# Turning prompt stick-breaking probabilities by a store, a fetch of 32x32 squares and VectorE, where TensorE turned them

## The reference, cut to what matters

```
def _sb_core(q, k, v, qpos, kpos):
    z = jnp.einsum('bqhd,bkhd->bhqk', q, k).astype(jnp.float32) * (SB_HD ** -0.5)
    valid = kpos[None, :] < qpos[:, None]
    log_beta = jax.nn.log_sigmoid(z)
    log_rem = jnp.where(valid, jax.nn.log_sigmoid(-z), 0.0)
    later = lax.cumsum(log_rem, axis=3, reverse=True) - log_rem
    a = jnp.where(valid, jnp.exp(log_beta + later), 0.0).astype(v.dtype)
    return jnp.einsum('bhqk,bkhd->bqhd', a, v)
...
    o = (o.reshape(b, s, SB_W) * jax.nn.silu(g)) @ w_out
```

## Time and profile before

| | |
|---|---|
| median of 3 runs | 806.83 us (806.25 to 807.87) |
| profiled execution, its own time | 809.91 us |
| span of the profiled execution | 808.1 us |
| TensorE busy | 775.6 us, 96% |
| VectorE busy | 548.2 us, 68% |
| ScalarE busy | 393.4 us, 49% |
| GpSimd busy | 207.7 us, 26% |

### The profile page before, as it was taken

The page is one execution under the profiler, slowest core; times in us unless marked ns, Lnnn a source line. Parts: engine busy times, 40 slices in busy tenths (PEclk is TensorE's granted clock), DMA queues, the critical chain, the costliest instruction groups (busy, mean ns, idle before and its releaser), DMA issues.

```text
span 808.1 us, 16622 instructions
## 1 busy us (share of the span) xinstructions
PE 775.6 (96%) x6364; PEld 679.1 (84%) x6364; DVE 548.2 (68%) x1086; ACT 393.4 (49%) x903; POOL 207.7 (26%) x301
## 2 busy tenths in 40 slices
PE   6999999999999998999999999999999999999895
PEld 5997788888889987778999988888888888777674
DVE  4476366666677669776923666776577777878778
ACT  3234533444534445332324556675567565687710
POOL 2020323211311231001340332233222343662003
PEclk9999999999999999999999999999999999999999
DMA  7632222311725354423243434334433444344113
GB/s 238 153 95 82 71 61 80 85 42 42 153 66 134 93 143 126 147 68 116 79 126 97 113 109 130 107 107 129 130 107 107 129 118 125 109 130 143 62 40 131
DMA packets 63869, 87.29 MB, mean 108 GB/s; under 512 B 8944, under 2 KB 48656, under 8 KB 63792
## 3 DMA queue, kind: packets, MB, share of 16 engines
q1 hardware_dynamic: 53216, 61.88, 25.8%
q0 software_dynamic: 10576, 24.34, 11.7%
HBM read 75.29 MB, written 10.90 MB: 107 GB/s over the span
## 4 chain that ended last, share of the span: by engine, by line
PE 72%; issue 10%; DVE 9%; ACT 4%; POOL 3%; DMA 2%; DVEq 0%; SPq 0%; ACTq 0%; POOLq 0%
PE turn L1020 26%; PE pair L1020 16%; PE value L1020 13%; PE proj L1020 10%; PE turn L1069 2%; POOL rstd L993 1%; POOL k_c L925 1%; DVE probs L1789 1%; PE proj L1231 1%; PE turn L1231 1%; PE proj L1069 1%; PE value L1069 1%; DVE w_words L1658 1%; PE pair L1069 1%; DVE xT_lo L1663 1%
## 5 line engine op out<-in xcount | busy, mean ns | idle before, releaser
L1020 PE MATMUL turn<-w_words,xT_hi 128*128 128x256 f32 (+2 forms) x696 | 147.4, 308 | 1.9 <-ACT k_n L1583 0.9
L1658 DVE TENSOR_TENSOR w_words<-stage,w_words 128x512 fp32r<-128x512 f32 (+1 forms) x136 | 91.8, 682 | 83.7 <-ACT w_words L1432 83.6
L1020 PEld LDWEIGHTS turn<-w_words,xT_hi 128*128 128x128 f32 x696 | 111.7, 191 | 7.4 <-issue 1.6
L1020 PE MATMUL turn<-w_words,xT_lo 128*128 128x256 f32 (+2 forms) x356 | 106.4, 299 | 0.0
L925 POOL DMA_DIRECT2D k_c<-in_cache_sb_k_dram x128 | 82.8, 655 | 85.3 <-DVE k_cT L1773 79.7
L1432 ACT CAST w_words<-stage 128x512 fp32r<-128x512 f32 (+1 forms) x144 | 87.4, 617 | 29.0 <-DMA stage<-in_w_in_even_dram 14.1
L1020 PE MATMUL turn<-xT_hi,w_words 128*128 128x320 f32 x384 | 90.0, 314 | 0.0
L1020 PE MATMUL value<-w_words,xT_hi 128*128 128x256 f32 (+2 forms) x360 | 79.8, 315 | 1.4 <-DVE w_words L1658 1.3
L1020 PE MATMUL pair<-w_words,xT_hi 128*128 128x512 f32 (+2 forms) x272 | 71.6, 350 | 0.0
L1020 PE MATMUL proj<-w_words,xT_hi 128*128 128x256 f32 (+2 forms) x352 | 69.8, 297 | 0.6 <-DVE uq L1865 0.6
L1020 PEld LDWEIGHTS turn<-w_words,xT_lo 128*128 128x128 f32 x356 | 67.8, 190 | 2.5
(11 more groups left out here) (470 smaller groups left out, 1705.5 us busy)
## 6 DMA issues: line engine op xcount, KB each, us to landing
stage<-in_w_in_odd_dram SPq DMA_DIRECT2D x64, 256.0 KB, 2.8
stage<-in_w_in_even_dram SPq DMA_DIRECT2D x44, 256.0 KB, 3.0
k_c<-in_cache_sb_k_dram POOLq DMA_DIRECT2D x128, 64.0 KB, 2.4
v_c<-in_cache_sb_v_dram SPq DMA_DIRECT2D x32, 256.0 KB, 2.9
mlaK<-in_cache_diff_k_dram POOLq DMA_DIRECT2D x32, 128.0 KB, 3.9
mlaK<-in_cache_diff_v_dram SPq DMA_DIRECT2D x32, 128.0 KB, 3.8
stage<-in_w_out_even_dram SPq DMA_DIRECT2D x16, 256.0 KB, 3.0
stage<-in_w_out_odd_dram SPq DMA_DIRECT2D x16, 256.0 KB, 2.8
```

Of the source, the lines that this page charges most:

```text
L1020: return nc.tensor.matmul(o, l, r, start=first, stop=last)
L1658: v.tensor_tensor(piece(w_lo[:, sec % 2, words]), piece(stage[:, n % STAGES, :]), piece(w_hi[:, sec % 2, words].bitcast(F32)), ALU.subtrac ...
```

## The change

22 prompt steps of groups 0 to 2 (the prompt steps among the first 33 steps: all 8 of groups 0 and 1, and the first 6 of group 2) lose their `turn` and `turn2`. By tile they are 6 steps of tile 3, 5 of tile 2, 5 of tile 1 and 6 of tile 0, together 110 blocks of 128x128. In their place come three jobs: `spill`, in which SP stores the step's probabilities into a scratch area (a part of the output `y_prompt` that is written for good later); `fetch`, in which POOL loads them with four DMAs as squares into the buffer that the turned blocks had, and the queries are dealt out so that row 4r+m goes to column r of block m; and `unpack`, one VectorE transpose in place over both heads. `value` waits for `unpack`, and VectorE's gate product writes its columns back in the queries' order.

```diff
+def through_memory(steps):
+    return [s for s in steps[:33] if s[0] == "B"]
...
         jobs.append(("score", now))
+        if i >= 2 and steps[i - 2] in by_memory:
+            jobs.append(("fetch", steps[i - 2]))
         for bundle in fill[:1]:
             jobs += bundle
-        if i >= 2:
+        if i >= 2 and steps[i - 2] not in by_memory:
             s = steps[i - 2]
             jobs.append(("turn", s))
...
         jobs += later.pop(i, []) + tails.get(i, [])
         if i >= 3:
             s = steps[i - 3]
+            if s in by_memory:
+                jobs.append(("unpack", s))
             jobs.append(("value", s))
...
         if i >= 1:
             jobs.append(("weigh", steps[i - 1]))
+            if steps[i - 1] in by_memory:
+                jobs.append(("spill", steps[i - 1]))
         jobs.append(("stick", now))
...
+                if kind == "spill":
+                    s = job[1]
+                    sp.wait_ge(stick_done, stick_no[s])
+                    sp.dma_start(scratch(s).rearrange("(q h n) -> q h n", q=P, h=2), stick_view(s)).then_inc(spilled[by_memory_no[s] % 4], 16)
...
+                if kind == "fetch":
+                    s = job[1]
+                    pool.wait_ge(spilled[by_memory_no[s] % 4], 16 * ((by_memory_no[s] + 3) // 4))
+                    if stick_no[s] > 2:
+                        wait_filled(pool, ("value", sb_steps[stick_no[s] - 3]))
+                    for e in range(P // SQ):
+                        pool.dma_start(packed(s)[e * SQ:(e + 1) * SQ].rearrange("r (x c) -> r x c", c=SQ),
+                                       scratch(s).rearrange("(r x e c) -> e r x c", r=SQ, e=P // SQ, c=SQ)[e]).then_inc(
+                                           fetched[by_memory_no[s] % 2], 16)
...
-                        wait_drained(pe, ("turn2", s))
+                        if s in by_memory_no:
+                            pe.wait_ge(squares_unpacked, by_memory_no[s])
+                        else:
+                            wait_drained(pe, ("turn2", s))
...
+                elif kind == "unpack":
+                    s = job[1]
+                    dve.wait_ge(fetched[by_memory_no[s] % 2], 16 * (P // SQ) * ((by_memory_no[s] + 1) // 2))
+                    v.transpose(packed(s), packed(s)).then_inc(squares_unpacked, 1)
...
-                    v.tensor_tensor(oT[:, 2 * g + blk, tok(t)], ps(job)[:, 0:P], gT[:, g % 2, blk, tok(t)], ALU.mult).then_inc(done, 1)
+                    o, values, gate = oT[:, 2 * g + blk, tok(t)], ps(job)[:, 0:P], gT[:, g % 2, blk, tok(t)]
+                    if job[1] in by_memory_no:
+                        o, gate = (x.rearrange("p (r m) -> p m r", m=4) for x in (o, gate))
+                        values = values.rearrange("p (m r) -> p m r", m=4)
+                    v.tensor_tensor(o, values, gate, ALU.mult).then_inc(done, 1)
```

More of the change, by code:

```diff
@@ L149, in stick_pipeline @@
     samples = [j for j, s in enumerate(steps) if s[0] == "BS"]
+    by_memory = through_memory(steps)
     for i, now in enumerate(steps):
@@ L593, in trunk_kernel @@
         keys_turned = sem("keys_turned")
+        squares_unpacked = sem("squares_unpacked")
+        spilled = [sem(f"spilled{i}") for i in range(4)]
+        fetched = [sem(f"fetched{i}") for i in range(2)]
         vc_in = [sem(f"vc_in{i}") for i in range(2)]
@@ L633, in turned, with packed, unpacked, scratch @@
             return wT1[:, nth[s] % 2, i, :] if s in stick_no else wT0[nth[s] % 2][i]
+        def packed(s):
+            n = 2 * width(s)
+            return flat(work8).rearrange("p (s n) -> p s n", s=2)[:, nth[s] % 2, 0:n]
+        def unpacked(s, h, j):
+            return packed(s).rearrange("p (m h j r) -> p h j m r", m=4, h=2, r=SQ)[:, h, j]
+        def scratch(s):
+            n = 2 * width(s)
+            base = by_memory_no[s] % 4 * P * D
+            return out[0].rearrange("b t d -> (b t d)")[base:base + P * n]
         def stick_view(s):
@@ L705, in trunk_kernel @@
                 units.setdefault(sec, [j, j])[1] = j
+        by_memory = [j[1] for j in schedule if j[0] == "spill"]
+        by_memory_no = {s: i + 1 for i, s in enumerate(by_memory)}
         stick_no = {s: i + 1 for i, s in enumerate(sb_steps)}
@@ L930, in _ @@
                 kind = job[0]
-                if job == ("uq", S_TILE, 1):
+                if kind == "fetch":
[7 more added lines that the diff above has]
+                                           fetched[by_memory_no[s] % 2], 16)
+                elif job == ("uq", S_TILE, 1):
                     wait_filled(pool, job)
@@ L1243, in _ @@
                     wait_bank(pe, job)
-                    wait_drained(pe, ("turn", s))
+                    if s not in by_memory_no:
+                        wait_drained(pe, ("turn", s))
                     o, w = ps(job), turned(s, 0)
@@ L1286, in _ @@
                                 c0 = (2 * blk + h) * HD
-                                m = mm(o[HD * h:HD * h + HD, 0:P], v_n[:, g % 2, j, c0:c0 + HD],
-                                       wT1[:, nth[s] % 2, h, tok(j)], j == 0, j == last)
+                                weights = unpacked(s, h, j) if s in by_memory_no else wT1[:, nth[s] % 2, h, tok(j)]
+                                m = mm(o[HD * h:HD * h + HD, 0:P], v_n[:, g % 2, j, c0:c0 + HD], weights, j == 0, j == last)
                     else:
@@ L1508, in _ @@
                         last = sb_steps[stick_no[s] - 4]
-                        wait_filled(act, ("turn2" if last[0] == "B" else "turn", last))
+                        if last in by_memory_no:
+                            act.wait_ge(spilled[by_memory_no[last] % 4], 16 * ((by_memory_no[last] + 3) // 4))
+                        else:
+                            wait_filled(act, ("turn2" if last[0] == "B" else "turn", last))
                     wait_filled(act, job)
```

## The result

| | before | after |
|---|---|---|
| median of 4 runs | 807.35 us (806.25 to 809.5) | 892.1 us (890.35 to 893.12) |
| span of the profiled execution | 808.1 us | 891.3 us |
| idle time of TensorE in the 36 steps | 4.0 us | 70.3 us |
| its mean granted clock over the span | 0.998 | 0.953 |

The changed kernel takes 1.1036 times as long (95% interval 1.102 to 1.1051): 84.7 us more, where 50.2 were forecast, and 892.1 us where 857 were, with a range up to 878. Slower was right, and so was the mechanism of the wait, VectorE's queue; the amount wasn't.

What follows compares the result with a forecast made beforehand. TensorE was taken to bound the kernel; +61.6 us of new waits, less 8.4 of turns and 3.0 of old idle time, gave +50.2 on 806.8, so 857 us, range 842 to 878.

Steps and rivals of the forecast that it cites:

- What bounds the kernel: In the 36 steps TensorE works 242.0 of 246.0 us; work removed gains its length, a new wait costs its full length.
- What TensorE loses: In the 22 steps, 110 blocks no longer turned at 0.108 us each: 11.9 us, of which 8.4 counted as kept.
- The wait that is added: Before the 22 values, TensorE waits for VectorE's queue to reach and finish the unpack: 61.6 us of new waiting.
- the sum: Over the 36 steps: +61.6 of waits, -8.4 of turns, -3.0 of old idle time, making +50.2 us.
- The unpack: VectorE's transposes before the 22 values, 1.29 us for tile 3 down to 0.37: 18.3 us, with nothing hiding it.
- Edits costed at nothing: ScalarE's copies, VectorE's added work, strided gate and value products, SP's spill and POOL's fetch: all taken as costing nothing.
- Is the round trip hidden?: Store and fetch for tile 3 take 9.1 us against 12.3 available in step 0: hidden, costing nothing.
- Clock 1.00 in the steps: Expected sign in the profile after: TensorE's granted clock stays at full speed through the 36 steps.
- a rival with a chance of 0.03: Waits of 4 us drop TensorE to 1.2 GHz for the step behind, in 11 steps: +70, 927 us; chance 0.03.

Runs made afterwards that it cites:

- a version that shows it bare: Changed kernel with each unpack moved forward in VectorE's queue, behind the score or the first bundle of the fill: 862.05 us, 1.0661 of before.
- the eleven-step version: Changed kernel with only the 11 steps of tiles 1 and 0 through memory, unpack early, behind the first bundle: 819.19 us, 1.0138 of before.
- the late eleven-step version: Changed kernel with only the 11 steps of tiles 1 and 0 through memory, unpack directly ahead of the value: 851.14 us, 1.0515 of before.
- the early fifteen-step one: Changed kernel with only tiles 1 and 0 plus steps 0, 3, 12 and 15 through memory, unpacks early: 830.21 us, 1.0265 of before.

## Why the prediction was wrong, step by step

- **What bounds the kernel.** Right. Leaving the turns out gave nearly microsecond for microsecond (13.7 for 11.9 + the idle time), and each new wait cost at least its full length.
- **What TensorE loses**, 0.108 us a block, 11.9 in all. Right; of the 13.7 measured without turns, 1.8 are idle relief. In the changed kernel all of the old 4.0 us of idle time went, as the 22 waits are all that is left; 3.0 were taken.
- **The wait that is added.** The mechanism was right and shown twice (narrow unpack; late against early place). The size nearly: 70.3 us of waits against 61.6. Of the 8.7 between them 3.5 are a matter of reckoning: the differences were taken from the old value's start, and TensorE now comes there 32 blocks of 0.108 us earlier. 2.3 more are the first step's wait for data. The 2.9 that remain are unexplained. Step by step, the waits of the eleven steps 3n+1 add up to 26.5 us against 26.7 forecast; the whole excess lies in the steps 3n. At full clock the whole difference was 862.2 - 808.35 = 53.9 us, 3.7 above the 50.2 of the sum.
- **The unpack**, 18.3 us: 7.5 + 4.9 + 3.5 + 2.6 = 18.5 measured, 1.25 us for 1024 columns. No cheaper and no dearer when wide or in place.
- **Edits costed at nothing.** The strided gate product takes 0.39 us in place of 0.29, behind TensorE's next score as said. The value that reads runs of 32 columns costs nothing extra (1.09 us for its 16 products, with the clock up). POOL and SP: nothing, by the run without the trip.
- **"Is the round trip hidden?"** Yes in 21 of 22 steps (the first waited 2.3 us), but the reason was weaker than it looked. The trip was put at 9.1 us and measured 13.1 in a version that shows it bare; the store alone took 3.8 us as the median for 512 KB (4.9 there), against the 2.6 of the earlier trace rows. In the step reckoned above it was hidden only because the steps had become so much longer. The Trainium skill, "DMA: Bandwidth & Descriptors", section "Latency and other measured facts", with some 2 us of fixed time a transfer, is borne out only as a floor: the smallest fetches (32 KB) landed in 2.1 us at the median; the spills took 2.4 to 5.7, at the median 3.5.
- **The step that failed: "Clock 1.00 in the steps".** The sum has no term for the clock. Its fall was kept as a rival with a chance of 0.03 and a price of +70, as another way in which things could go. It belonged in the sum, on top of the waits that the same text had just worked out: it measured 892.1 - 862.2 = 30 us. The row read against it was the only one at hand, the end of the kernel: idle from 800, clock at 1.00 up to 804. But the second row of that group, 0.53 on average from 804 to 808, was the warning: there the clock fell, and waits of up to 4 us, eleven of them, had just been worked out. Its price was too high. It took eleven steps with some 6.5 us of work each that would double, 70 us. Measured are 16 falls that cost 30 us together, 1.9 each: the two shown here cover 3.4 us ((1 - 0.57) x 4 / 0.5) and some 7 us, of which one lies within the wait, and each microsecond at half speed costs only half a microsecond. With the measured 30 in the sum, the forecast would have been 887.

All in all: 70.3 of waits, less the 4.0 of idle time that were there before and the 11.9 of turns, are +54.4, against 53.9 measured at full clock. With +30 for the clock it makes +84, of 84.7 measured. TensorE's busy time says the same of the clock without that run: it rose by 18.3 us though 11.9 us of turns had gone, so by 30.2.

**What stays open.** Why a spill takes 2.4 to 5.7 us to land where stores of like size took 2.0 to 2.6 us at other places; another queue did not shorten it, and contention with the loads beside it was not tried by itself. Also open are the 2.9 us of waits named above, which part of the eleven-step version's remaining loss is ScalarE's waits, and what decides whether the clock falls behind a wait of some 2 us.

## What to carry to other kernels

Work that is handed from a nearly full engine to a half idle one is paid by the place where it stands in that engine's queue, not by its length: before anything else, read when the new engine comes to that place and what it still has to do before it (the place alone was worth 32 us for 11 steps, with the clock behind the waits). Where the sum says that TensorE will stand still for several us at a time, put the lower clock of the work behind each stop into the same sum. And where one wait is removed, work out the next one bare, as a path of its own: no version through memory came under the kernel before, though turning on VectorE with the data at hand, stale as it was, did.

## What the runs showed of the hardware

- The granted clock after a stop, in the changed kernel: after the wait of 3.16 us that ended at 522.72 it was still 1.00 from 519 to 523 and then 0.57 from 524 to 528. In the one of 4.53 us it fell before the work began again, and was 0.50 for the 5 us from 539. So the fall can come after the work has resumed, which is why the gap itself looks harmless. It also came behind a shorter wait, of 2.21 us, that ended at 567.75 (third row):

```profile
519.00:523.00 4.00, 0.84 (x10) 0.60 (x10) 2.05 (x3) 1.90 (x3) 0.00 (x0) 1.00 0.26 77
524.00:528.00 4.00, 4.00 (x20) 4.00 (x18) 1.31 (x4) 1.26 (x3) 1.76 (x3) 0.57 0.25 81
568.00:573.00 5.00, 5.00 (x38) 4.61 (x35) 4.28 (x5) 1.22 (x3) 4.05 (x7) 0.66 0.29 79
```

- The length of the stop alone does not decide it. In the late eleven-step version two waits of the same 2.11 us, ended at 483.58 and 581.53, with equally much work around them, left the clock at 1.00 the one time and brought it down the other:

```profile
481.00:491.00 10.00, 7.89 (x82) 7.35 (x81) 5.17 (x9) 4.16 (x9) 2.87 (x5) 1.00 0.50 129
579.00:589.00 10.00, 7.89 (x70) 7.06 (x69) 4.90 (x9) 4.16 (x9) 4.72 (x8) 0.83 0.49 127
```

- Throwaway turns of the identity, 549 of them in 22 waits, kept the clock at 1.00 and won 30 us, without being of any use to the result.
- The scatter over runs was smallest with the clock kept up (0.5 us) and largest in the early fifteen-step one (11.5), with 2.8 in the changed kernel and 6.5 in the early eleven-step one. But a lowered clock does not by itself bring scatter: the changed kernel without the trip ran at 0.953 to 0.955 and spread by 1.2.
